# Head norms of a hybrid mixer: sums of squares over partitions as two products of a high and a low part

## What is computed

```python
def rmsnorm(x, g):
    xf = x.astype(jnp.float32)
    y = xf * lax.rsqrt(jnp.mean(xf * xf, axis=-1, keepdims=True) + EPS)
    return (y * g.astype(jnp.float32)).astype(x.dtype)

o_a = rmsnorm(o_a, hg_norm).reshape(B, T, HG_VD) * jax.nn.silu(hg)
o_b = rmsnorm(o_b, gla_norm).reshape(B, T, GLA_VD) * jax.nn.silu(gr)
return jnp.concatenate([o_a, o_b], axis=-1) @ w_out
```

## Time and profile before

| | |
|---|---|
| median of three runs | 1200.69 us |
| profiled execution | 1199.81 us |
| its span in the trace | 1198.1 us |
| TensorE busy | 1166.8 us, 97% |
| VectorE busy | 808.8 us, 68% |
| ScalarE busy | 624.6 us, 52% |
| GpSimd busy | 120.2 us, 10% |
| sums over partitions (line 2021) | 16 passes, two to a head, from 127.1 to 286.6 us |

### The profile page before, as it was taken

One profiled execution on the slowest core, in us unless ns is written; L12 is line 12 of the kernel. 1 busy time (PEld: TensorE's weight loads), 2 busy tenths in 40 slices (PEclk: granted clock), 3 DMA queues, 4 the chain that ended last, 5 costly groups with the idle time before them and its releaser, 6 DMA issues.

```text
span 1198.1 us, 16327 instructions
## 1 busy us (share of the span) xinstructions
PE 1166.8 (97%) x5851; PEld 963.2 (80%) x5851; DVE 808.8 (68%) x1232; ACT 624.6 (52%) x1161; POOL 120.2 (10%) x129
## 2 busy tenths in 40 slices
PE   6999999999999999999999999999999999999997
PEld 5777788887888888888888877777978888888886
DVE  4466867885666687678477367864577687668474
ACT  5553655554656355545445766554555544545431
POOL 2222311310021112120000000100000000000000
PEclk9999999999999999999999999999999999999999
DMA  4331122124413332332232232202423232231221
GB/s 129 105 87 54 54 59 66 53 89 141 164 58 104 123 105 88 105 123 71 71 106 85 66 91 60 73 34 88 158 81 105 96 123 87 88 122 53 88 88 70
DMA packets 87490, 108.18 MB, mean 90 GB/s; under 512 B 9186, under 2 KB 48195, under 8 KB 87428
## 3 DMA queue, kind: packets, MB, share of 16 engines
q1 hardware_dynamic: 85684, 101.85, 27.1%
q0 software_dynamic: 1744, 5.51, 1.4%
HBM read 104.20 MB, written 2.10 MB: 89 GB/s over the span
## 4 chain that ended last, share of the span: by engine, by line
PE 83%; DVE 8%; ACT 6%; issue 2%; DMA 1%; POOL 0%; DVEq 0%; SPq 0%; ACTq 0%
PE bank L1856 22%; PE bank L1858 22%; PE bank L1857 22%; PE pp L1857 2%; PE pp L1858 2%; PE pp L1856 2%; PE po L2336 2%; PE pp L1998 1%; PE pp L1901 1%; DVE w_lo L610 1%; ACT w_hi L601 1%; PE pp L2317 1%; ACT w_hi L599 1%; PE po L2009 0%; PE misc L1858 0%
## 5 line engine op out<-in xcount | busy, mean ns | idle before, releaser
L1856 PE MATMUL bank<-h_lo,w_hi 128*128 128x512 f32 (+4 forms) x764 | 292.9, 383 | 8.6 <-DVE h_lo L1321 4.1
L1858 PE MATMUL bank<-h_hi,w_hi 128*128 128x512 f32 (+4 forms) x764 | 289.9, 379 | 0.0
L1857 PE MATMUL bank<-h_hi,w_lo 128*128 128x512 f32 (+4 forms) x764 | 289.7, 379 | 0.0
L1856 PEld LDWEIGHTS bank<-h_lo,w_hi 128*128 128x128 f32 (+1 forms) x764 | 142.5, 187 | 39.1 <-issue 5.1
L1858 PEld LDWEIGHTS bank<-h_hi,w_hi 128*128 128x128 f32 (+1 forms) x764 | 142.5, 186 | 27.2
L1857 PEld LDWEIGHTS bank<-h_hi,w_lo 128*128 128x128 f32 (+1 forms) x764 | 142.6, 187 | 25.7
L1856 PE MATMUL bank<-wx,a_hl 128*128 128x512 f32 x320 | 125.4, 392 | 0.1
L599 ACT CAST wx<-raw 128x1024 fp32r<-128x1024 f32 x72 | 74.6, 1049 | 96.1 <-DVE raw L1551 64.9
L1858 PE MATMUL bank<-wx,a_hl 128*128 128x512 f32 x320 | 124.6, 389 | 0.0
L1857 PE MATMUL bank<-wx,a_hl 128*128 128x512 f32 x320 | 124.5, 389 | 0.0
L1562 DVE TENSOR_TENSOR y<-y,bank 128x512 f32<-128x512 f32 x80 | 54.7, 684 | 87.4 <-PE bank L1858 87.3
(11 more groups left out here) (364 smaller groups left out, 2166.8 us busy)
## 6 DMA issues: line engine op xcount, KB each, us to landing
stage<-in_mlp_w SPq DMA_DIRECT2D x66, 512.0 KB, 3.7
raw<-in_mlp_w SPq DMA_DIRECT2D x50, 512.0 KB, 3.5
stage<-in_ev_w_in SPq DMA_DIRECT2D x28, 512.0 KB, 3.8
spare<-in_mlp_w SPq DMA_DIRECT2D x12, 512.0 KB, 4.6
stage<-in_ev_w_out SPq DMA_DIRECT2D x8, 512.0 KB, 3.5
stage<-in_od_w_out SPq DMA_DIRECT2D x8, 512.0 KB, 3.5
stage<-in_od_w_in SPq DMA_DIRECT2D x10, 256.0 KB, 2.9
x_tok<-in_x SPq DMA_DIRECT2D x4, 512.0 KB, 5.4
```

The lines of the kernel that those rows point to most:

```text
L1856: nc.tensor.matmul(dst, wh, xl_, start=first, stop=False)
L1857: nc.tensor.matmul(dst, wl, xh, start=False, stop=False)
L1858: return nc.tensor.matmul(dst, wh, xh, start=False, stop=last)
```

## The change

The squares of a head are written twice by ScalarE: once in float32 as before and once rounded to fp32r (sq_hi). A new step on VectorE, `square_low`, subtracts the two and writes the rest as fp32r over the float32 squares (sq_lo lies where sq[:, 0, :] lies, sq_hi where rinv[:, 0, :] lies). TensorE sums with two fp32r products, of sq_lo and of sq_hi, added up in the same bank, in place of the plain float32 product. The all-ones matrix becomes fp32r, and its other uses read it as float32. The semaphore o_sq now counts three steps to a head. In VectorE's walk through the slots `square_low` stands one slot after SQUARES, behind the evacuation of that slot's tile and ahead of head_gate. The buffers sq and rinv move behind tmp and tok in memory; the total size is the same.

```diff
-        ones = sb("ones", [P, P])
+        ones = sb("ones", [P, P], F32R)
...
-        sq = sb("sq", [P, 2, T])
         tmp = sb("tmp", [P, 2, T])
-        rinv = sb("rinv", [P, 2, T])
         tok = sb("tok", [P, 16, NT])
...
+        with ExitStack() as sums:
+            sq = sb("sq", [P, 2, T], F32, sums)
+            rinv = sb("rinv", [P, 2, T], F32, sums)
+        with ExitStack() as sums:
+            sq_lo = sb("sq_lo", [P, T], F32R, sums)
+            sb("beside_sums", [P, T], F32, sums)
+            sq_hi = sb("sq_hi", [P, T], F32R, sums)
+        sb("under", [P, 4, T])
...
                 nc.scalar.activation(sq[:, 0, :], po[:, :], ACT.Square).then_inc(o_sq, 1)
+                nc.scalar.activation(sq_hi[:, :], po[:, :], ACT.Square).then_inc(o_sq, 1)
                 nc.scalar.activation(sq[:, 1, :], po[:, :], ACT.Copy).then_inc(o_read, 1)
...
+            def square_low(o):
+                dve.wait_ge(o_sq, 3 * o + 2)
+                nc.vector.tensor_tensor(sq_lo[:, :], sq[:, 0, :], sq_hi[:, :].bitcast(F32), ALU.subtract).then_inc(o_sq, 1)
...
                 if i == IDLE_SLOT:
                     split_low(dve, EO + SPLIT - 1)
+                for o in SQUARES[i - 1] if i >= 1 else ():
+                    square_low(o)
                 for o in MIXES[i]:
                     head_gate(o)
...
             def head_sum(o):
-                pe.wait_ge(o_sq, o + 1)
+                pe.wait_ge(o_sq, 3 * o + 3)
                 pe.wait_ge(o_read, o + 1)
-                nc.tensor.matmul(po[:, :], ones[:, :], sq[:, 0, :], start=True, stop=True).then_inc(o_sum, 1)
+                nc.tensor.matmul(po[:, :], ones[:, :], sq_lo[:, :], start=True, stop=False)
+                nc.tensor.matmul(po[:, :], ones[:, :], sq_hi[:, :], start=False, stop=True).then_inc(o_sum, 1)
```

More of the change, by code:

```diff
@@ L759, in _ @@
         def _(pool):
-            nc.gpsimd.memset(ones[:, :], 1.0).then_inc(consts_ready, 1)
+            nc.gpsimd.memset(ones[:, :].bitcast(F32), 1.0).then_inc(consts_ready, 1)
             nc.gpsimd.memset(eps[:, :], EPS).then_inc(consts_ready, 1)
@@ L1426, in cumulate @@
                     s = slice(c * P, (c + 1) * P)
-                    ins = nc.vector.tensor_tensor_scan(b_sb[:, s], ones[:, :], t_f[:, s], 0.0, ALU.mult, ALU.add)
+                    ins = nc.vector.tensor_tensor_scan(b_sb[:, s], ones[:, :].bitcast(F32), t_f[:, s], 0.0, ALU.mult, ALU.add)
                 ins.then_inc(b_ready, 1)
+            def square_low(o):
+                dve.wait_ge(o_sq, 3 * o + 2)
+                nc.vector.tensor_tensor(sq_lo[:, :], sq[:, 0, :], sq_hi[:, :].bitcast(F32), ALU.subtract).then_inc(o_sq, 1)
             def head_gate(o):
@@ L1906, in _ @@
             for h, g_bank in ((0, po), (1, misc)):
-                ins = nc.tensor.matmul(g_bank[:, :], ones[0:1, :], grow[:, h * T:(h + 1) * T], start=True, stop=True)
+                ins = nc.tensor.matmul(g_bank[:, :], ones[0:1, :].bitcast(F32), grow[:, h * T:(h + 1) * T], start=True, stop=True)
             ins.then_inc(gain_ready, 1)
```

## The result

The changed kernel's median is 1204.52 us (1203.56 to 1206.84, 8 runs) against 1200.86 us for the kernel before in the same comparison (8 runs). The ratio is 1.0031, with a 95% interval of 1.0021 to 1.0042, so the change makes the kernel 3.7 us slower (2.5 to 5.0). Its profiled execution took 1204.47 us with a span of 1202.7.

What follows compares the result with a forecast made beforehand. TensorE's matmul stream plus whatever holds it up was taken to bound the kernel. Head 1 +4.1 (containing head 0's 0.60), then -0.1 -0.4 +0.5 +0.5 -0.4 -0.4, gave +3.8 on 1200.69: 1204.5 us, 8-in-10 range 1202.4 to 1207.4.

Steps and rivals of the forecast that it cites:

- the clock rival: TensorE's clock falls to half behind head 1's gap of about 4 us: 1.7 to 3 us more, 1206 to 1207.5; chance 0.22.
- What the product costs: On TensorE, two split-format products take 0.46 us for the plain product's 0.86, saving 0.40 a head where it doesn't wait.
- Head 0: The subtraction pushes VectorE's unbroken row by 0.60 us, so TensorE resumes 0.60 later at the masked copies.
- Head 1: The subtraction stands behind slot 22's weight split on VectorE; TensorE waits about 4 us for it: +4.1, including head 0's 0.60.
- my first sign of being right: TensorE waits some 4 us before the sum of head 1, released by VectorE's new line.
- Heads 2 to 7: Head 2 -0.1, head 3 -0.4, heads 4 and 5 +0.5 each through ScalarE's longer chain, heads 6 and 7 -0.4 each.
- The split pair: Rival: the pair takes the old 0.86 us, heads 1, 2, 3, 6 and 7 each 0.3 to 0.4 dearer, 1206.2; chance 0.05.
- given back behind head 1: Rival: TensorE's later waits of 1.5, 1.4 and 1.6 us absorb the +4.1, time 1200.3; chance 0.04.

Runs made afterwards that it cites:

- head 1 alone: Only head 1 takes the new fp32r pair sum, the other heads keep the old one; against the kernel before: ratio 1.0039, +4.7 us (3.1 to 6.2).
- high-part kernel: Changed kernel with VectorE's subtraction and the low part's product left out, one fp32r square and one product per head; against the kernel before: ratio 0.9977, -2.8 us.
- the changed kernel (again): The changed kernel measured and profiled once more, nothing altered; against the kernel before: ratio 1.0047, +5.6 us (3.7 to 7.7).
- no new head: All heads keep the old sum, only the ones matrix's type and the places of sq and rinv change; against the kernel before: ratio 1.0003, +0.3 us.

## Why the prediction was right

**The number.** 1204.5 was forecast, 1204.52 measured. The agreement to 0.1 us is chance: the difference of the two medians has an interval of 2.5 us, and the second comparison of the same kernel gave +5.6 us (3.7 to 7.7). What is borne out is "some 4 us slower", and the steps. There is luck in the base as well, to which the clock rival below comes back.

**What the product costs: right.** In the first profile after, the work behind head 3's sum came 0.40 earlier against before than the work ahead of it, and so it was at head 4. The pair in a running stream is 0.46 (195.10, 195.32, next at 195.55).

**Head 0: right in its step, wrong in its cover.** The push of 0.60 is there (1.15 in the trace with the race won; 2.90 against 1.91 with it lost, which again is 0.60 and the 0.40). I had said that GpSimd had nothing running where the subtractions land. That is true, but three products behind the subtraction it has, and which engine is held up there decides 1.75 us. I took a single outcome from the trace of before for the rule. Of the twelve traces seven show the other, among them unchanged work. How often the kernel before loses it no trace shows; its times suggest that it does (see the clock rival).

**Head 1: right, and the whole of the loss.** +4.1 was forecast; 4.1 is the reading by the start mark in the second trace, alone it measures +4.7 (3.1 to 6.2), and without it the change is +1.0, or +0.5 when the subtraction stands 3.3 us earlier. The wait itself, my first sign of being right, was forecast as 4 us and showed 1.9 and 2.5. TensorE's list is late by other causes ahead of it, and the position behind it is set by VectorE, which TensorE's lateness reached in one of the four traces with head 1's new sum (the 0.37 of head 1 alone). A wait's length tells how early the waiting engine was; the cost is the position of what follows.

**Heads 2 to 7: right.** 0.86 turned into 0.79 at head 2 was forecast; the lateness against before changes by 0.07 over it (5.91 to 5.84). With head 1 on the old sum TensorE comes earlier and waits 0.34 at head 2's, so that it costs 0.2 there. At head 4 the work behind the wait of 2.39 is 0.45 later than before, for 0.48 forecast. At head 5 it is 0.44, but not by the one wait growing, as I wrote: that stays at 1.4, and two small new ones (0.35 and 0.21) stand ahead of it. At heads 6 and 7 the 0.40 each is there in the first profile after (lateness 7.89 to 7.45 between the two sums, and 7.05 at the last wait), and head 7 had its subtraction in time.

**The clock rival: it took place, at another gap.** I gave it 0.22 and looked for it behind head 1's wait of 4 us. It fell there once (behind 2.53), but in all ten traces in which TensorE waited 0.79 us or more behind head 0 it fell there, and in neither of the two with 0.16. It doesn't go by the length of the wait alone: behind the 2.4 us ahead of head 5 (2.2 in the high-part kernel) it fell in four traces and not in two, and behind waits of 1.5 us at that place in none of six, nor behind the last one of 1.6. The Trainium skill, TensorE: Matmul & The Clock Gate, "HAM oscillation — how this bites in real kernels", speaks of gaps longer than these; where it says that gaps bring the slow rate, the traces agree, but the length isn't borne out, with falls behind 0.79 and 1.15.

So the clock is part of the measured difference. Laid beside each other with the race won, the changed kernel (again) has 240.2 in the table for 233.4: +6.8, of which 3.8 are the forecast's and 3.0 two falls. With the race lost it has 240.5 for the 236.2 of no new head, which stands in for before here: +4.3, of which 0.5 are the clock, as both have a fall that costs. From the start mark to the end of the span the two pairs give +6.3 and +3.9. That is one trace for each. The mean granted clocks of single executions show the mixture behind the medians: 19 of 90 executions of the kernel before have 0.999, as the first trace without a fall, and a median time of 1199.6 us; 26 have 0.998 and 1201.6; 22 have 0.995 or less. (The mean holds falls near the start too.) All 13 of the changed kernel have 0.993 to 0.995. So the base of 1200.69 to which I added 3.8 already held slower executions than the trace from which I took the steps, in all likelihood with a lost race and a fall, and the changed kernel's falls stand against them. The steps are right; that their sum alone gave the time, with nothing for a clock that does fall, is luck. What share of +3.7 and of +5.6 is the clock's stays open.

**The other rivals fell.** The split pair is cheaper (-2.8 for the product alone). Nothing was given back behind head 1: the distance stays at +5.9 in the first trace until the next step of the sum.

## What to carry to other kernels

A new step is priced by its place in the queue of its engine, not by its duration: 0.6 us of VectorE cost 4 us at the one head at which the consumer stands a slot closer, and next to nothing 3.3 us earlier in the same list. When work is added by a rule over a table (here one slot after the squares), look for the entry at which the rule's distance is smaller than at the others. And before two profiles are compared, look for places at which the same work shows two outcomes, and measure from a mark ahead of the change.

## What was not expected of the hardware

Where VectorE's products of two SBUF operands and GpSimd's subtraction meet, one of the two is held up, and which it is changes between executions of one kernel: the changed kernel lost in its first profile and won in its second. VectorE's product took 0.42 or 1.33 us. GpSimd's start was 0.16 to 0.19 us ahead of it in the seven traces with the longer time and 0.13 to 0.17 in the five with the shorter. The Trainium skill, SBUF — State Buffer, "SBUF: two separate sides", describes this as an exclusive lock that the first to start holds for its whole instruction. The traces agree that one waits for the other's end (125.48 + 1.22 = 126.70, VectorE's end at 126.98). But GpSimd started first in all twelve by the trace and was the one held up in five, so the recorded starts don't tell who will win.

TensorE's clock fell to half behind waits as short as 0.79 us at one place of this kernel, and not behind 1.6 at another, and cost 1.1 to 2.3 us each time that no wait hid it. A long fall may be hidden: in the first profile after, TensorE lost some 1.9 us to it between 139 and 150 and then waited that much less for the subtraction.
